# RWKV inverse of the 32-row squares: x and its transpose added in one instruction, an idle product ahead of each set

## The reference, cut to what matters

```python
def rwkv7_time_mix(h, ...):
    ...
    kk = kk / max(norm(kk), 1e-12)
    k = k * (1.0 + (a - 1.0) * k_a)
    decay = exp(-exp(w_log))
    y = wkv7_scan(r, decay, k, v, -kk, kk * a)     # state S, one token after the other
    yn = layer_norm_of_each_head(y) * lnx_g + lnx_b
    bonus = sum(r * k * r_k) * v
    return ((yn + bonus) * g) @ w_o
```

## Time and profile before

| what | value |
|---|---|
| median of three executions | 2059.43 us |
| profiled execution, its own time | 2062.8 us |
| its span in the profile | 2060.8 us |
| PE busy | 1979.1 us, 96% of the span |
| DVE busy | 1047.0 us, 51% |
| ACT busy | 944.5 us, 46% |
| POOL busy | 1298.6 us, 63% |
| mean granted PE clock | 0.96 of 2.4 GHz |

### The profile page before, as it was taken

How to read it: one execution, slowest core, us unless ns; L and a number is a source line. 1 busy time by engine, 2 the same in 40 slices (tenths; PEclk the granted TensorE clock), 3 DMA queues, 4 the chain that set the end, 5 groups by cost and what they waited for, 6 DMA issues and landing times.

```text
span 2060.8 us, 47633 instructions
## 1 busy us (share of the span) xinstructions
PE 1979.1 (96%) x19284; PEld 1879.4 (91%) x19284; DVE 1047.0 (51%) x1638; ACT 944.5 (46%) x1698; POOL 1298.6 (63%) x528
## 2 busy tenths in 40 slices
PE   8999997899899999999999899999999999999998
PEld 8999787777699999999996899999999988999998
DVE  5881577445468834873277487312181336334431
ACT  5343553222243344334456534444356665656553
POOL 6888362000068787888760588978665755677886
PEclk9999999688799999999998899999999999999999
DMA  7445332000044454445430255554445432454552
GB/s 283 164 176 190 116 110 83 3 4 4 2 149 179 173 179 161 174 173 182 147 140 22 103 184 183 197 181 167 147 161 191 150 137 103 144 185 143 183 189 97
DMA packets 40999, 291.53 MB, mean 141 GB/s; under 512 B 4496, under 2 KB 5776, under 8 KB 5904
## 3 DMA queue, kind: packets, MB, share of 16 engines
q1 hardware_dynamic: 40560, 288.12, 39.1%
q10 hardware_dynamic: 288, 1.18, 0.2%
HBM read 288.23 MB, written 1.05 MB: 140 GB/s over the span
## 4 chain that ended last, share of the span: by engine, by line
PE 33%; issue 27%; POOLq 18%; POOL 18%; DVE 2%; ACT 2%; DMA 0%; DVEq 0%; SPq 0%; ACTq 0%
POOLq L2152 18%; POOL w_low L2148 18%; PE ps L640 10%; PE ps L648 10%; PE ps L644 10%; PE ps L1478 1%; PE ps L1465 1%; PE ps L1455 1%; ACT units L2054 0%; POOLq L2147 0%; DVE units L2174 0%; DMA X<-x_in 0%; ACT units L1549 0%; ACT w_high L1549 0%; PE ps L799 0%
## 5 line engine op out<-in xcount | busy, mean ns | idle before, releaser
L2148 POOL TENSOR_TENSOR w_low<-wring,w_high 128x1024 fp32r<-128x1024 f32 x524 | 1298.4, 2493 | 745.5 <-ACT w_high L1549 714.1
L640 PE MATMUL ps<-in_high,w_high 128*128 128x256 f32 (+1 forms) x2808 | 812.5, 289 | 13.1 <-POOL w_low L2148 6.5
L648 PE MATMUL ps<-in_high,w_low 128*128 128x256 f32 (+1 forms) x2808 | 803.7, 286 | 0.0
L644 PE MATMUL ps<-in_low,w_high 128*128 128x256 f32 (+1 forms) x2808 | 801.8, 286 | 0.0
L1549 ACT ACTIVATE w_high<-wring 128x1024 fp32r<-128x1024 f32 x524 | 542.1, 1055 | 243.8 <-PE ps L640 239.1
L640 PEld LDWEIGHTS ps<-in_high,w_high 128*128 128x128 f32 x2808 | 533.2, 190 | 24.7 <-issue 14.5
L648 PEld LDWEIGHTS ps<-in_high,w_low 128*128 128x128 f32 x2808 | 533.5, 190 | 0.0
L644 PEld LDWEIGHTS ps<-in_low,w_high 128*128 128x128 f32 x2808 | 532.5, 190 | 0.4
L640 PE MATMUL ps<-hid_high,w_high 128*128 128x272 f32 (+1 forms) x880 | 250.6, 285 | 0.0
L648 PE MATMUL ps<-hid_high,w_low 128*128 128x272 f32 (+1 forms) x880 | 250.5, 285 | 0.0
L644 PE MATMUL ps<-hid_low,w_high 128*128 128x272 f32 (+1 forms) x880 | 250.0, 284 | 0.0
(11 more groups left out here) (369 smaller groups left out, 2595.8 us busy)
## 6 DMA issues: line engine op xcount, KB each, us to landing
wring<-stream SPq DMA_DIRECT2D x270, 1024.0 KB, 4.8
con<-consts SPq DMA_DIRECT2D x1, 2055.0 KB, 15.7
X<-x_in SPq DMA_DIRECT2D x1, 1088.0 KB, 7.6
units<-decay ACTq DMA_DIRECT2D x1, 1024.0 KB, 5.0
out<-AL SPq DMA_DIRECT2D x4, 256.0 KB, 2.4
AL<-stream SPq DMA_DIRECT2D x2, 256.0 KB, 19.0
par<-params SPq DMA_DIRECT2D x1, 187.0 KB, 5.5
con<-consts ACTq DMA_DIRECT2D x1, 130.0 KB, 5.6
```

The costliest lines, as they stand in the source:

```text
L640: mm = pe.matmul(o, wh, high(k), start=(k == 0), stop=False)
L644: mm = pe.matmul(o, wh, low(k), start=False, stop=False)
L648: mm = pe.matmul(o, wl, high(k), start=False, stop=(k == kt - 1))
L2148: pool.tensor_tensor(w_low[:, (half + h) % SPLIT_RING, :], wring[:, slot, h * HALF * P:(h + 1) * HALF * P], w_high[:, (half + h) % SPLIT_R ...
```

## The change

Three things are done.

1. x and xt of a chunk now lie side by side in one tile (`rk_both`, two halves), for even and odd groups apart. The results of `rk_merge`, o and ot, lie side by side in one PSUM bank too (`rk_merged_bank`). At levels where both are needed DVE adds them with one instruction of 256 numbers in place of two of 128. `rk_x{c}_added` counts once a level, and both `rk_under` and, through it, `rk_merge` of the next level stand behind this one addition.
2. The bank that this frees (3) takes an idle product, `fill(IDLE_BANK, 1)`, ahead of the sets of chunks 1 and 2: of `rk_under` at levels 2, 3 and 4, and of `rk_merge` at levels 1 to 5. That makes 16 in a group, 64 in all. It stands ahead of the set's waits.
3. The fill ahead of each of the three level 0 sets of the first group has 8 products in place of 4.

```diff
-        RK_COUNT = [2 * n - 3 for n in RK_LEVELS]
+        RK_COUNT = [n - 1 if n < LEVELS else n for n in RK_LEVELS]
...
-        rk_xt, rk_x, rk_ym = (even[9:12], beside_levels[3:6]), even[12:15], beside_levels[0:3]
+        rk_both, rk_ym = (even[9:12], beside_levels[0:3]), beside_levels[3:6]
+        rk_x, rk_xt = ([[v[:, i, :, :] for v in both] for both in rk_both] for i in range(2))
...
+        RK_LEVEL_BANK, IDLE_BANK = (4, 0, 2), 3
...
+        def rk_merged_bank(c):
+            C, B = CHUNKS[c][1], RK_SIDE[c]
+            return ps[0:C, RK_LEVEL_BANK[c], 4 * B:12 * B].rearrange("p (i q t) -> p i q t", i=2, q=4)
...
             def rk_under(g, c, n):
-                    pe.wait_ge(S[f"rk_x{c}_added"], g * RK_COUNT[c] + 2 * n - 2 - (c > 0))
+                    pe.wait_ge(S[f"rk_x{c}_added"], g * RK_COUNT[c] + n - 1)
...
             def rk_merge(g, c, n):
-                if n > 1:
-                    pe.wait_ge(S[f"rk_x{c}_added"], g * RK_COUNT[c] + 2 * n - 2)
+                if n == LEVELS - 1:
+                    pe.wait_ge(S[f"rk_x{c}_added"], g * RK_COUNT[c] + n)
...
             def rk_levels(g):
                         if g == n == 0:
-                            fill(4, 4)
+                            fill(4, 8)
+                        elif 1 < n < LEVELS - 1 and c:
+                            fill(IDLE_BANK, 1)
...
                     for c in chunks if n else ():
+                        if n < LEVELS - 1 and c:
+                            fill(IDLE_BANK, 1)
                         rk_merge(g, c, n)
...
             # DVE
                         dve.wait_ge(S[f"rk_merge{c}_ready"], g * (RK_LEVELS[c] - 1) + n)
-                        o, ot = rk_level_bank(c, 1), rk_level_bank(c, 2)
                         if n < RK_LEVELS[c] - 1:
-                            tt(rk_x[c][0:C, :, :], o, rk_x[c][0:C, :, :], ALU.add).then_inc(S[f"rk_x{c}_added"], 1)
-                        tt(xt[c][0:C, :, :], ot, xt[c][0:C, :, :], ALU.add).then_inc(S[f"rk_x{c}_added"], 1)
+                            both = rk_both[g % 2][c][0:C, :, :, :]
+                            ins = tt(both, rk_merged_bank(c), both, ALU.add)
+                        else:
+                            ins = tt(xt[c][0:C, :, :], rk_level_bank(c, 2), xt[c][0:C, :, :], ALU.add)
+                        ins.then_inc(S[f"rk_x{c}_added"], 1)
```

More of the change, by code:

```diff
@@ L341, in build @@
         even = carve(group, *[(6, P)] * 3, *[(4, 2, C) for C in sizes] * 2,
-                     *[(4, B) for B in RK_SIDE] * 2, *[(4, HALF_ROWS)] * 4, (6, P),
+                     *[(2, 4, B) for B in RK_SIDE], *[(4, HALF_ROWS)] * 4, (6, P),
                      *[(4, HALF_ROWS)] * 2)
-        beside_levels = carve(in_parts, *[(4, B) for B in RK_SIDE] * 2, (2, T), (2, T), (4, HD), (4, HD), *[(4, 2, N_META)] * 2,
+        beside_levels = carve(in_parts, *[(2, 4, B) for B in RK_SIDE], *[(4, B) for B in RK_SIDE], (2, T), (2, T), (4, HD), (4, HD), *[(4, 2, N_META)] * 2,
                               *[(4, HALF_ROWS)] * 4, *[(4, HALF_ROWS)] * 2)
@@ L347, in build @@
             (T1[:, :, :], [(4, 2, P)] * 2), (T2[:, :, :], [(4, 2, P)] * 2), (A[:, 24:32, :], [(6, P)] * 2))]
-        rk_tm = (even[0:3], [even[19], *odd[2]])
+        rk_tm = (even[0:3], [even[16], *odd[2]])
         rk_lb = (even[3:6], [beside_levels[10], odd[0][0], odd[1][0]])
         rk_lk = (even[6:9], [beside_levels[11], odd[0][1], odd[1][1]])
-        rk_xt, rk_x, rk_ym = (even[9:12], beside_levels[3:6]), even[12:15], beside_levels[0:3]
+        rk_both, rk_ym = (even[9:12], beside_levels[0:3]), beside_levels[3:6]
+        rk_x, rk_xt = ([[v[:, i, :, :] for v in both] for both in rk_both] for i in range(2))
         rk_square, rk_root, rk_z, rk_sa = beside_levels[6:10]
-        rk_joined, rk_below = [None, *even[20:22]], [None, *beside_levels[16:18]]
-        rk_upper = [[None, *v] for v in (even[15:17], beside_levels[12:14])]
-        rk_lower = [[None, *v] for v in (even[17:19], beside_levels[14:16])]
+        rk_joined, rk_below = [None, *even[17:19]], [None, *beside_levels[16:18]]
+        rk_upper = [[None, *v] for v in (even[12:14], beside_levels[12:14])]
+        rk_lower = [[None, *v] for v in (even[14:16], beside_levels[14:16])]
         rk_mid, rk_mid_exp, rk_end, rk_ends, states = carve(small, (3, 8), (3, 8), (3, 8), (2, 8, 2), (4, 2, HD))
@@ L435, in build, with rk_level_bank, rk_late_bank @@
         TB = slice(N_META, T)
[L437 to L442, removed]
+        RK_LEVEL_BANK, IDLE_BANK = (4, 0, 2), 3
+        def rk_level_bank(c, i):
+            C, B = CHUNKS[c][1], RK_SIDE[c]
+            return ps[0:C, RK_LEVEL_BANK[c], 4 * B * i:4 * B * (i + 1)].rearrange("p (q t) -> p q t", q=4)
+        def rk_late_bank(c, i, B):
+            return ps[:, RK_LEVEL_BANK[c] + i, 4 * B:8 * B].rearrange("p (q t) -> p q t", q=4)
+        def rk_merged_bank(c):
+            C, B = CHUNKS[c][1], RK_SIDE[c]
+            return ps[0:C, RK_LEVEL_BANK[c], 4 * B:12 * B].rearrange("p (i q t) -> p i q t", i=2, q=4)
         def rk_banks(g, c):
@@ L879, in rk_under @@
                 else:
-                    pe.wait_ge(S[f"rk_x{c}_added"], g * RK_COUNT[c] + 2 * n - 2 - (c > 0))
+                    pe.wait_ge(S[f"rk_x{c}_added"], g * RK_COUNT[c] + n - 1)
                 settle(C)
-                lb, x = rk_lb[g % 2][c], rk_x[c]
-                o = rk_level_bank(c, 0, HALF_ROWS if n == LEVELS - 1 else RK_SIDE[c])
+                lb, x = rk_lb[g % 2][c], rk_x[g % 2][c]
+                o = rk_late_bank(c, 0, HALF_ROWS) if n == LEVELS - 1 else rk_level_bank(c, 0)
                 for q in range(4):
@@ L905, in rk_merge @@
                 o, ot, xt, y = rk_level_bank(c, 1), rk_level_bank(c, 2), rk_xt[g % 2][c], rk_ym[c]
-                if n == LEVELS - 1:
-                    ot = rk_level_bank(c, 2, HALF_ROWS)
+                if n >= LEVELS - 2:
+                    ot = rk_late_bank(c, 1, HALF_ROWS if n == LEVELS - 1 else BLOCK)
                 for q in range(4):
@@ L1751, in rk_assemble @@
             def rk_assemble(g, c):
-                x, xt, upper, lower = rk_x[c], rk_xt[g % 2][c], rk_upper[g % 2][c], rk_lower[g % 2][c]
-                act.wait_ge(S[f"rk_x{c}_added"], g * RK_COUNT[c] + 8)
+                x, xt, upper, lower = rk_x[g % 2][c], rk_xt[g % 2][c], rk_upper[g % 2][c], rk_lower[g % 2][c]
+                act.wait_ge(S[f"rk_x{c}_added"], g * RK_COUNT[c] + LEVELS - 3)
                 copy(rk_joined[c][FOURTH[0], :, FIRST], x[FOURTH[0], :, :])
@@ L1869, in _ @@
                     act.wait_ge(S[f"rk_under{c}_ready"], g * RK_LEVELS[c] + 1)
[L1870 removed]
+                    copy(rk_x[g % 2][c][0:CHUNKS[c][1], :, :], rk_level_bank(c, 0)).then_inc(S[f"rk_x{c}_begun"], 1)
                 for c in range(3):
```

6 lines of the change are left out of this document (3 added, 3 removed).

## The result

The changed kernel takes 2065.49 us, the median of 20 executions (2057.99 to 2073.78), against 2059.95 us of the kernel before in 20 executions on the same chip. The ratio is 1.0028, with an interval of 1.0015 to 1.0042. Timed again in a later series it was 1.0042 (1.0027 to 1.0057). So it is 5.5 to 8 us slower: no change by the prediction's bound of 0.5%, but a loss, as both intervals lie above 1. The forecast was 2070. The ratios of this document leave out executions in the chip's slower state; among all of them that is one, of 2085.80 us, in the run with two additions and late products.

What follows compares the result with a forecast made beforehand. PE was taken to bound the levels, so added products are mostly paid for: 19.8 + 0 + 0 - 8.8 = +11.0 us, giving a median of 2070 us. The range was 2047 to 2082, the likeliest case's own 2064 to 2080.

Steps and rivals of the forecast that it cites:

- the prediction's bound of 0.5%: Whole kernel: anything within 0.5%, 10.3 us, of 2059.4 us was taken as no change; chance of that 0.36.
- the falls at the start of groups 2 to 4: Clock drops at 400.1, 451.3 and 499.1 us, claimed to stay because no idle product stands before them.
- the last stretch: Half-clock stretch of 30.7 us from 523.0 us, levels 4 and 5 of the last group; cut by two thirds, as one possibility.
- rival 1: Idle products in the levels hold PE's clock: 76 us of half clock go, sum -10.6 us, 2049 us; chance 0.22.
- The joint addition at 0: DVE's one addition in place of two in the levels: costs 0, with ends of -2.6 and +3.9 us.
- The start fills at 0: Three longer fills at the first group's start, 12 products: hidden behind DVE, cost 0, or 1.3 us if uncovered.
- The number of products: Idle products added in the levels: 64, two falling into idle time, leaving 62 to be paid for.
- The price of a product: One idle product in the levels: 0.27 us at full clock, 0.50 at half, 0.37 by share; 62 cost 22.9 us.
- The idle time that swallows them: PE's waits in the levels: 1.5 us before scores and turns, 1.6 us of issue waits, leaving products at 19.8 us.
- the two products that I had put in idle time: Ahead of the first group's level 1 merges, in PE's 5.06 us of idle; claimed to cost nothing.
- Rival 2: Fills in the levels find more idle time, 9 us of them falling in: +2 us, 2061 us; chance 0.28.
- The clock: Slow stretches in the levels get 22 us shorter in all, at 0.40 each giving back 8.8 us.

Runs made afterwards that it cites:

- two additions and late products: Kernel with idle products only at levels 4 and 5 of the last group, x and xt added by two instructions instead of one: 2054.10 us, 0.9962.
- the eight late products: Changed kernel keeping only the last group's idle products at levels 4 and 5, start fills back at four: 2047.96 us (0.9946), again 2051.63 us (0.9961).
- eight at the start: Kernel with only the last group's idle products at levels 4 and 5, its three start fills left at eight instead of four: 2050.77 us, 0.9956.

## Why the forecast came out as it did

- **The mechanism held in the main.** PE bounds the levels; the products are paid for except where PE was idle; the falls at the start of groups 2 to 4 stay; half clock stays over 60 us in all. The forecast had the last stretch cut by two thirds or the first one shortened by as much. Both happened, and more: the last one is gone in the first profile, and the first one went from 27.3 to 13.7 us. So one sign of rival 1, that no stretch is left where the last one was, was met; the other, less than 50 us at half clock, was not. The groups did not get 4 to 6 us longer each: -1.4, +4.6, +7.9 and -6.0.
- **The joint addition at 0** was right: 0.9998 alone. Its row is 128x256, x16 + x16 = 32, at 421 ns against the 410 foreseen, and PE has no wait before `rk_under` behind it.
- **The start fills at 0** were right as far as can be seen.
- **The number of products was wrong**: 72 in the levels and not 64, so 70 to be paid for and not 62.
- **The price of a product was too low.** The step "1.09 us for four, 0.27 each" divided a row of four. All but the start fills are single ones, and a single one takes 0.42 us and not 0.27, or 0.72 and not 0.50. In the changed kernel's timeline 22 of the 72 stand at half clock. The 70 take 34.5 us from their starts to the next set's, 0.49 each, in place of 22.9 us: 3.9 us of the difference are the eight too few, 7.7 the price.
- **The idle time that swallows them was taken too small.** For these products I took 1.5 + 1.6 = 3.1 us. The groups' idle time shrank by 15.5 us; 2.2 of that go to the two longer start fills that lie in the windows and 0.8 to the two products that I had put in idle time, which leaves 12.5. What PE still waits for in the changed kernel between 366 and 536 us (us in total, times, longest), the rows that answer to the earlier trace rows:

```profile
PE ps L977 <- issue: 1.5, 2, 1.0
PE ps L877 <- DVE AL L2191: 1.1, 2, 0.6
...
PE ps L877 <- DVE group L2191: 0.6, 1, 0.6
```

  The waits of the scores (L877, L864 before) went from 4.3 us to 1.7. I had 1.5 us for them. Half of the 15.5 comes from the first group, 11.9 us idle before and 4.2 after, and 3.9 from the last. The five rows are 8.5 us, where the whole list has 15.0. The list also ends at 523 us, in the middle of the longest wait behind the first group, the 2.26 us that end at 524.07. Counting length less busy for each whole group would have given the 30 us that there were. Rival 2 had named this: 9 us, with the words that 12.1 us of idle are in the windows.
- **The clock** gave back about twice what I took. It is 34.0 us less at half clock inside the groups, where I had 22. What that is worth is left over when the busy time is accounted for: 35.3 us for the 72, 2.2 for the start fills, 20.6 measured, so 16.9 us, 0.50 for each of the 34.0. In the last group alone, the busy time changed by 70.22 - 72.33 = -2.1 us with 18 products more (9.2 us) and 23.8 us less at half clock: 11.3 / 23.8 = 0.47. Both are over the 0.40 that I took and the 0.46 that I had as the upper bound.

On this footing the terms come to 34.5 - 12.5 - 16.9 = +5.1 us, which is the groups' measured difference; as the clock's term is a remainder, that is a balance and not a test. Against the forecast the products cost 11.6 us more, idle time swallows 9.4 more, and the clock gives back 8.1 more: 11.0 + 11.6 - 9.4 - 8.1 = +5.1. So it is in part luck that the forecast came near. With its 22.9 us for the products, and idle time and clock as measured, the sum would have been 22.9 - 12.5 - 16.9 = -6.5 us, faster. Rival 2, the fills finding more idle time, was right in its mechanism; with 22.9 us for the products it gave 2061, on the other side of what was measured.

Still open: what decides whether the late slow stretch comes, and how long it lasts (30.7 and 3.4 us in two profiles of the eight late products, none with eight at the start), and why the stretch at the start of the second group lasts 13.7 us in one profile and 41.0 in another.

## What to carry to other kernels

- Price an inserted product as a single one between the neighbours that it will have. A row of four of the same kind hides that the first costs nearly twice what each further one does (0.42 and 0.22 us here).
- Take PE's idle time over each whole stage (length less busy) before you say what a filler can fall into; a list of the largest waits shows only a part of it.
- Test idle products place by place. Here 8 of 72 gained 8 to 12 us over none and the 54 of the first three groups cost 13.5 us.
- Count the inserted instructions in the first profile before you divide by their number; the page's record counts gave it here.

## What was not expected of the hardware

- Busy time as the profile counts it did not bring the clock back soon. In the changed kernel the stretches at half clock from 399.1, 453.7 and 508.4 us are 13.70 of 13.70, 20.50 of 20.50 and 17.10 of 17.10 us busy. Before, the same stretches were 17.1, 13.7 and 10.2 us, with PE idle for part of them: 51.3 us in all with PE always busy, 41.0 with idle time in between.
- In one execution a stretch of 41.0 us at half clock, with PE busy for 39.12. It is from the first series of the eight late products, in its second group, in which it has no added product; the second series of the same kernel has some 17 us there:

```profile
400.30:441.30 41.00, 39.12 (x894) 31.31 (x896) 12.28 (x35) 4.69 (x13) 0.00 (x0) 0.50 0.01 3
```

  So a profile of one execution can't tell what a change does to one stretch; here only the medians and the stretches that came or went in several kernels did.
